# First expert layer of a two-block network on Trainium2: token rows made by one-hot products on TensorE, in place of gathers from a token store

## What is computed

```python
def _hier_moe(h, w_group, b_group, w_router, b_router, w_gate, w_up, w_down):
    ...                                       # eid: 2 experts of each token; wts: their weights
    order = jnp.argsort(eid)
    dest = pad_start[eid_s] + jnp.arange(n_asg) - start[eid_s]
    xb = h_pad[tok_buf].reshape(n_blocks, MOE_BLOCK, d)      # rows of h, expert by expert
    def expert_block(args):
        xe, e = args
        return (jax.nn.silu(xe @ w_gate[e]) * (xe @ w_up[e])) @ w_down[e]
    y = lax.map(expert_block, (xb, blk_e)).reshape(cap, d)
    out = jax.ops.segment_sum(y.astype(jnp.float32) * w_buf[:, None], tok_buf, num_segments=t + 1)
    return out[:t]
```

## Time and profile before

| | us |
|---|---|
| median of 3 runs (lowest, highest) | 2401.6 (2398.14, 2402.22) |
| span of the profiled execution, core 0 | 2400.5 |
| its whole time | not listed apart from the three runs |
| PE busy | 2173.3 (91%) |
| DVE busy | 1108.4 (46%) |
| ACT busy | 692.3 (29%) |
| POOL busy | 215.8 (9%) |
| mean granted TensorE clock | 0.952 of full |

### The profile page before, as it was taken

How to read it: one execution, slowest core, us unless ns; L and a number is a source line. 1 busy time by engine, 2 the same in 40 slices (tenths; PEclk the granted TensorE clock), 3 DMA queues, 4 the chain that set the end, 5 groups by cost and what they waited for, 6 DMA issues and landing times. The chain is left out here.

```text
span 2400.5 us, 29499 instructions
## 1 busy us (share of the span) xinstructions
PE 2173.3 (91%) x11404; PEld 1361.6 (57%) x11404; DVE 1108.4 (46%) x1760; ACT 692.3 (29%) x1102; POOL 215.8 (9%) x330
## 2 busy tenths in 40 slices
PE   7999999998899999988898888888788899999996
PEld 5778788876777888856633333333366533333332
DVE  5677655465676456577511111111587522222223
ACT  4243344344334443366111110110237111111110
POOL 2000000010000001100111111111120000000000
PEclk9989999999999999999799999998889899999998
DMA  8745576573655657501799999999830799999995
GB/s 295 260 151 190 193 235 202 184 277 135 226 206 193 211 171 248 163 2 39 301 335 401 411 409 411 406 408 411 302 84 8 299 380 428 428 428 429 428 428 230
DMA packets 175600, 656.73 MB, mean 274 GB/s; under 512 B 16295, under 2 KB 61943, under 8 KB 150288
## 3 DMA queue, kind: packets, MB, share of 16 engines
q1 hardware_dynamic: 159648, 622.65, 67.6%
q0 software_dynamic: 14032, 30.00, 4.0%
q10 hardware_dynamic: 1824, 2.73, 0.3%
HBM read 649.97 MB, written 23.79 MB: 281 GB/s over the span
## 5 line engine op out<-in xcount | busy, mean ns | idle before, releaser
L750 PE MATMUL bank<-sb_ring_rounded,sb_hT_rounded 128*128 128x512 f32 x2432 | 605.7, 397 | 18.7 <-DVE sb_ring_rounded L2045 8.4
L1382 PE MATMUL bank<-sb_ring,sb_arena 128*64 128x512 f32 x1984 | 491.1, 640 | 94.1 <-DMA sb_ring<-in_w_up 91.3
L750 PEld LDWEIGHTS bank<-sb_ring_rounded,sb_hT_rounded 128*128 128x128 f32 x2432 | 459.4, 191 | 119.5 <-issue 12.9
L1382 PEld LDWEIGHTS bank<-sb_ring,sb_arena 128*64 128x64 f32 x1984 | 152.4, 146 | 378.7 <-issue 372.9
L2045 DVE TENSOR_TENSOR sb_ring_rounded<-sb_ring,sb_ring_rounded 128x2048 fp32r<-128x2048 f32 (+1 forms) x142 | 314.9, 2258 | 112.4 <-ACT sb_ring_rounded L1516 107.4
L750 PE MATMUL bank<-sb_ring_rounded,sb_arena_rounded 128*128 128x512 f32 x1408 | 356.8, 395 | 7.6 <-DVE sb_arena_rounded L2032 7.0
L1516 ACT ACTIVATE sb_ring_rounded<-sb_ring 128x2048 fp32r<-128x2048 f32 x146 | 268.1, 1887 | 125.7 <-PE bank L750 100.1
L750 PEld LDWEIGHTS bank<-sb_ring_rounded,sb_arena_rounded 128*128 128x128 f32 x1408 | 266.1, 190 | 63.3 <-DVE sb_arena_rounded L2032 7.3
L1926 ACT ACTIVATE sb_hb<-bank 64x512 f32<-64x512 f32 x64 | 37.8, 590 | 697.4 <-PE bank L1382 697.4
L1406 PE MATMUL bank<-sb_ring,sb_arena 128*64 128x512 f32 x1008 | 233.4, 606 | 3.5 <-DVE sb_arena L2877 3.5
L2877 DVE COPY sb_arena<-bank 128x256 f32<-128x256 f32 x64 | 27.1, 424 | 319.2 <-PE bank L1393 319.1
(11 more groups left out here) (372 smaller groups left out, 2121.9 us busy)
## 6 DMA issues: line engine op xcount, KB each, us to landing
sb_ring<-in_w_down SPq DMA_DIRECT2D x63, 2048.0 KB, 22.0
sb_ring<-in_w_up SPq DMA_DIRECT2D x62, 2048.0 KB, 21.3
sb_ring<-in_w_gate SPq DMA_DIRECT2D x62, 2048.0 KB, 16.9
sb_ring<-in_w_ada SPq DMA_DIRECT2D x48, 1024.0 KB, 7.5
sb_ring<-in_ffn_w_gu SPq DMA_DIRECT2D x44, 1024.0 KB, 7.8
sb_ring<-in_xa_w_kv SPq DMA_DIRECT2D x16, 1024.0 KB, 7.3
sb_ring<-in_ffn_w_down SPq DMA_DIRECT2D x16, 1024.0 KB, 6.4
sb_ring<-in_od_w_in SPq DMA_DIRECT2D x12, 1024.0 KB, 7.7
```

The source lines that it names most:

```text
L750: ins = pe.matmul(bank[b][0:rows, :], rnd(x), rnd(w[:, k, :]), start=start and k == k0 and q == 0, stop=stop and k == k1 - 1 and q == len( ...
L1382: ins = pe.matmul(bank[2 * j + part][part * ROWS:(part + 1) * ROWS, :], mxT[:, j, k, :], w[:, k, :], start=k == 0, stop=k == KD - 1)
```

## The change

Layer 0 makes its rows as layer 1 does. The store of tokens, the gathers, their waits and the turned single steps go. The marks of layer 0 cover four token tiles: 16 places for each partition in place of 8, made in two halves, the sums of which lie in the tiles `silu` and `fix`. Each half of the 1024 columns then takes four products, not two. The tiles `bc`, `tokens`, `silu` and `fix` get a plain and a rounded name at the same address. Outputs of layer 0 are collected in `hb[0]` and `bc[1]` (the last two steps in `tokens`), since the old place is used by the resident tokens' marks. As `bc[1]` is now in use during the loop, the fills of `bc[0]` and `bc[1]` for the next layer move from the start of layer 0 into its last pair (`next_modulation`). The second index table, which was for gathers, goes in both layers. GpSimd's descriptor scratch is 4096 bytes of each partition.

```diff
+        def places_of(l):
+            return st[:, 72:80 if l else 88].rearrange("p (q s) -> p q s", s=2)
+        def marks_of(t):
+            return silu_s[:].rearrange("p k c -> p (k c)")[:, t * P:(t + 1) * P] if t < 2 else fix[:, t - 2, :]
+        def my_of(l, j, own=False):
+            if l == 1:
+                return view(6144, 2, D)[0:ROWS, j, :]
+            return tokens[0:ROWS, j, :] if own else hb[0:ROWS, 0, :] if j == 0 else bc[0:ROWS, 1, :]
...
-                    sp.wait_ge(m["rows0"], 16)
-                else:
...
-                    claim(T0)
-                    claim(T1)
-                    place_rows(0)
+                claim(T0)
+                claim(T1)
+                place_rows(l, 0)
...
-            def place_rows(i):
-                m = moe[1]
+            def place_rows(l, i):
+                m = moe[l]
                 pe.wait_ge(m["marked"], i + 1)
                 pe.sem_inc(s["passed"], 1)
                 for half in range(2):
-                    for t in range(2):
-                        ins = pe.matmul(bank[T0 + half], place_marks[:, t, 0, :, :].rearrange("p s n -> p (s n)"), hr[:, t, half * NB:(half + 1) * NB],
-                                        start=t == 0, stop=t == 1)
+                    cols = slice(half * NB, (half + 1) * NB)
+                    if l == 0:
+                        for t in range(4):
+                            ins = pe.matmul(bank[T0 + half], marks_of(t), hr[:, t, cols], start=t == 0, stop=t == 3)
+                    else:
+                        for t in range(2):
+                            ins = pe.matmul(bank[T0 + half], place_marks[:, t, 0, :, :].rearrange("p s n -> p (s n)"), hr[:, t, cols],
+                                            start=t == 0, stop=t == 1)
                     ins.then_inc(m["pe_xT"], 1)
...
-                def turn_rows(j, e, landed_rows):
-                    pe.wait_ge(m[f"rows{j}"], landed_rows * 16)
-                    pe.sem_inc(s["passed"], 1)
-                    for k in range(KD):
-                        ins = pe.transpose(bank[T0 + j][:, k * ROWS:(k + 1) * ROWS], mx[0:ROWS, j, k:D:KD], ident[0:ROWS, 0:ROWS])
-                    ins.then_inc(m["pe_xT"], 1)
-                if l == 1:
-                    turn_placed(0)
+                turn_placed(l, 0)
...
-                        if l == 0 and not (last and j == 1):
-                            turn_rows(1 - j, e + 1, i + 1 + j)
-                        if l == 1 and not last:
-                            (place_rows, turn_placed)[j](i + 1)
+                        if not last:
+                            (place_rows, turn_placed)[j](l, i + 1)
...
-                        act.dma_start(DR["tok"][t * P:(t + 1) * P, :], hr[:, t, :]).then_inc(s[f"tok_stored{t % 2}"], 16)
...
-                    zeros = cst[:, C_WIN0:C_WIN0 + P].unsqueeze(1).to_broadcast([P, 2 * KD, P])
-                    act.activation(view(0, 2 * KD, P), zeros, ACT.Copy).then_inc(s["rows_zeroed"], 1)
...
+                rows_out(0)
+                placed_turned(0)
...
-            def mark(i):
-                m = moe[1]
+            def mark(l, i):
+                m = moe[l]
+                places = places_of(l)
                 if not (isinstance(i, int) and i == 0):
                     dve.wait_ge(m["marked"], i)
                     dve.tensor_scalar(places, places, -2.0 * ROWS, None, ALU.add).then_inc(m["places"], 1)
                     dve.wait_ge(m["places"], i)
                     dve.wait_ge(m["pe_xT"], i * 4 - 2)
                 row = cst[:, C_ROW:C_ROW + ROWS].unsqueeze(1).to_broadcast([P, 8, ROWS])
-                at = places.rearrange("p q s -> p (q s)").unsqueeze(2).to_broadcast([P, 8, ROWS])
-                dve.tensor_tensor(place_marks.rearrange("p t j s n -> p (t j s) n"), row, at, ALU.is_equal).then_inc(m["equals"], 1)
-                dve.wait_ge(m["equals"], i + 1)
-                dve.tensor_tensor(place_marks[:, :, 0, :, :], place_marks[:, :, 0, :, :], place_marks[:, :, 1, :, :], ALU.add).then_inc(m["marked"], 1)
+                flat = places.rearrange("p q s -> p (q s)")
+                equal = place_marks.rearrange("p t j s n -> p (t j s) n")
+                if l == 1:
+                    dve.tensor_tensor(equal, row, flat.unsqueeze(2).to_broadcast([P, 8, ROWS]), ALU.is_equal).then_inc(m["equals"], 1)
+                    dve.wait_ge(m["equals"], i + 1)
+                    dve.tensor_tensor(place_marks[:, :, 0, :, :], place_marks[:, :, 0, :, :], place_marks[:, :, 1, :, :], ALU.add).then_inc(m["marked"], 1)
+                    return
+                for half in range(2):
+                    at = flat[:, 8 * half:8 * half + 8].unsqueeze(2).to_broadcast([P, 8, ROWS])
+                    if half:
+                        dve.wait_ge(m["equals"], i * 3 + 2)
+                    dve.tensor_tensor(equal, row, at, ALU.is_equal).then_inc(m["equals"], 1)
+                    dve.wait_ge(m["equals"], i * 3 + 2 * half + 1)
+                    to = (silu_s[:].rearrange("p k c -> p (k c)") if half == 0 else fix[:].rearrange("p t n -> p (t n)"))
+                    to = to.rearrange("p (t s n) -> p t s n", t=2, s=2)
+                    dve.tensor_tensor(to, place_marks[:, :, 0, :, :], place_marks[:, :, 1, :, :], ALU.add)\
+                       .then_inc(m["marked"] if half else m["equals"], 1)
...
-                    step(dve.tensor_scalar(places[:, :, 1], mtmp[:, 3, 64:68], float(ROWS), -float(ROWS * N_EXP), ALU.mult, ALU.add))
-                    step(dve.tensor_tensor(places[:, :, 1], places[:, :, 1], rank, ALU.add))
-                    step(dve.scalar_tensor_tensor(places[:, :, 0], whole_blocks, float(ROWS * (N_EXP - 1)), places[:, :, 1], ALU.mult, ALU.add))
-                    step(dve.tensor_scalar(places[:, :, 1], places[:, :, 0], -float(ROWS), None, ALU.add))
-                    mark(0)
+                places = places_of(l)
+                step(dve.tensor_scalar(places[:, :, 1], mtmp[:, 3, 64:64 + J], float(ROWS), -float(ROWS * N_EXP), ALU.mult, ALU.add))
+                step(dve.tensor_tensor(places[:, :, 1], places[:, :, 1], rank, ALU.add))
+                step(dve.scalar_tensor_tensor(places[:, :, 0], whole_blocks, float(ROWS * (N_EXP - 1)), places[:, :, 1], ALU.mult, ALU.add))
+                step(dve.tensor_scalar(places[:, :, 1], places[:, :, 0], -float(ROWS), None, ALU.add))
+                mark(l, 0)
...
-                dve.tensor_scalar(idx[:, 1, :], idx[:, 0, :], 1, None, ALU.logical_shift_right).then_inc(*c.up(s["idx_ready"]))
-                settle()
+                dve.sem_inc(s["idx_ready"], 1)
...
-            def gather(j, e):
-                since(pool, m["pe_xT"], e - 1)
-                apart()
-                if isinstance(e, int):
-                    pool.sem_inc(m["picked_in"], 1)
-                    at = column(1, e)
-                else:
-                    pool.tensor_copy(pick[:, 0, j:j + 1], column(1, e)).then_inc(m["picked_in"], 1)
-                    pool.wait_ge(m["picked_in"], e + 1)
-                    apart()
-                    at = pick[:, 0, j:j + 1]
-                pool.indirect_dma_start(out=mx[0:ROWS, j, :], out_offset=None, in_=DR["tok"],
-                                        in_offset=bass.IndirectOffsetOnAxis(ap=at, axis=0),
-                                        bounds_check=tiles * P - 1, oob_is_err=False).then_inc(m[f"rows{j}"], 16)
...
-                        gather(j, i * 2 + j + 2)
                     if not opening(i):
                         pool.wait_ge(m[f"stored{j}"], i * 16)
@@ -3093,12 +3056,14 @@
                         pool.sem_inc(s["y_stored"], 1)
                         for t in range(2):
                             pool.wait_ge(s[f"y_loaded{t}"], 16)
+                    if l == 0 and last and j == 1:
+                        pool.wait_ge(m["pe_xT"], i * 4 + 2)
+                        apart()
+                        next_modulation()
                     if not (opening(i) and j == 0) and not (own and j == 1):
-                        store(1 - j, i * 2 + j - 1)
-            if l == 0:
-                gather(0, 0)
-                gather(1, 1)
+                        store(1 - j, i * 2 + j - 1, last and j == 1)
...
                 fill(2, mod(l, 0, 5))
-                if l == 0:
+                if l == 1:
+                    fill(0, I["g_final_2"])
+                def next_modulation():
                     fill(0, mod(1, 0, 1))
                     fill(1, mod(1, 0, 0))
-                else:
-                    fill(0, I["g_final_2"])
-                if l == 0:
-                    pool.wait_ge(s["rows_zeroed"], 1)
-                experts(pool, c, step, l)
+                experts(pool, c, l, next_modulation)
...
-    nc = bacc.Bacc("TRN2", target_bir_lowering=False, num_devices=1)
+    nc = bacc.Bacc("TRN2", target_bir_lowering=False, num_devices=1, dynamic_dma_scratch_size=4096)
```

134 lines of the change are left out of this document (50 added, 84 removed).

## The result

The changed kernel takes 2386.64 us (median of 4 runs, 2385.80 to 2391.94) against 2399.87 for the kernel before (4 runs). The ratio is 0.9949, with a 95% interval of 0.9935 to 0.9964. It is faster, by 13.2 us between the medians and 12.2 (8.6 to 15.6) by the ratio, where 7.4 were forecast. The profiled execution took 2391.94 us, with a span of 2390.1 (2400.5 before).

What follows compares the result with a forecast made beforehand. Transfers were taken to bound layer 0's pairs (32.38 us), TensorE afterwards (30.80). Loop -11.6, start +1.9, end +2.6 and layer 1 -0.3 sum to -7.4 us: 2394.2 us from 2401.6, range 2388.5 to 2401.

Steps and rivals of the forecast that it cites:

- Other edits: Outside loop and seams: one shift less in layer 1, -0.3 us; rows of y and smaller descriptor scratch cost nothing.
- rival d: More than forecast: expert 0 starts at 1206, fills land early; -10.8 us, 2390.8 us; chance 0.12.
- The loop: Layer 0, expert 0 to expert 31: pairs of 30.80 us set by TensorE, 480.7 to 469.0 us, -11.6.
- The start: Before layer 0's expert 0: placing replaces token stores and first gather, partly at low clock; +1.9 us, range +0.9 to +2.7.
- The end: End of layer 0: VectorE waits for the moved modulation fills before the norm; +2.6 us, range +1.1 to +5.5.
- Layer 1: The index table loses a shift in layer 1, one VectorE operation before the step count: -0.3 us.
- (a): Seams of layer 0: fills land with the median or later, placing begins at low clock; -3.7 us, 2397.9; chance 0.17.
- (b): Layer 0's loop: transfers stay the bound at 31.5 us a pair; -2.4 us, 2399.2; chance 0.11.
- (c): Layer 0's loop: placing waits for marks' second half, clock falls; at 1.7 us a pair +18, 2420; chance 0.10.
- Layer 0 at 31.1: Mild form of transfers staying the bound: weights at 435 GB/s, 32 stored rows 1.1 us, layer 0's pair 31.1 us.

Runs made afterwards that it cites:

- b_scratch4k: The kernel before with only GpSimd's descriptor scratch set to 4096 bytes: 2394.3 us against 2399.06, ratio 0.9978.
- a_again: The changed kernel run once more with no edit: 2386.35 us, ratio to the kernel before 0.9953.
- the second profile: Profile of the changed kernel run again without an edit: span 2384.1 us, profiled at 2385.94 us.
- b_half_gather: The kernel before with gathers of half rows, 2 KB for each index instead of 4 KB (leaves work out): 2386.87 us in one run.
- b_no_gather: The kernel before without layer 0's gathers beyond the first two (leaves work out): 2364.72 us in one run.

## Why the prediction was wrong

**The step that failed** is in "Other edits": "GpSimd's smaller descriptor scratch costs nothing as long as only a store and two fills are outstanding". I looked for a loss only, in the loop, and put the edit at nothing. It gives 6.1 us in the profiles and 5.3 (3.1 to 7.4) by the ratio of b_scratch4k, at the end of the program, where GpSimd's drain held the exit open. The trace of before had the row: a drain of 10.48 us and 6.3 us in which SyncE waited at the exit. I read the end of expert layer 0 and never the end of the program. With this term the sum is -12.7 to -13.5, and the time moved by 12.2 to 13.2. Without it, after against before with the small scratch is 0.9949 / 0.9978, 7.0 us; with a_again, timed beside b_scratch4k, it is 6.0 by the ratios and 8.0 by the medians. The sum had 7.4. That it is so near is in part luck, since its terms missed by up to 1.5 us in both directions, as follows. The range's near end, 2388.5, was built from the terms of the expert layer alone (rival d), so it could not hold the time.

**The loop**, -11.6: -13.0 measured. The mechanism was right: bound moved to TensorE, no waits, clock 1.00, marks in time. The pair was mis-sized by 0.2 us, since placing 16 records takes 7.07 us, not twice 3.63; over 14 pairs that is 2.8. The stretch from expert 0 to expert 2 took 1.5 us more than the 26.6 of the sum (1208.21 to 1236.35), because that row was from layer 1, whose first products ran at the full clock (7.09 us) and here took 8.78. That transfers would allow 30.4 was near (30.0 to 30.3), but the reasoning under it was wrong: I shared the 2.39 us between stores and gathers at 25 ns a row, and the gathers cost nearly all of it, 35 ns a row.

**The start**, +1.9: +2.5 from the rank's reduction and +2.8 in the second profile, just past the range's +2.7; +2.2 by expert 0's own start. The first placing did run at the low clock in part: it took 8.24 us, 1.0 more than the 7.26 of the sum and not 1.8. From its end to expert 0 it took 5.2 us where 3.39 + 1.1 were summed.

**The end**, +2.6: +3.6 in the first profile, +1.4 in the second, inside the range. The wait for the fills is as described (6.79 and 5.51 us). From the issue of the first fill to VectorE's start are 7.9 us (1700.23 to 1708.10) and 7.3 in the second profile; 7.75 were taken. For one fill the Trainium skill's fit (DMA: Bandwidth & Descriptors, "Anatomy of one DMA — SWDGE (gpsimd) path") gives an estimate of 3.2 us, and this case's traces don't agree: in the first profile after, GpSimd's transfers of the tile `bc` there took 6.0 to 8.7 us to land. The second profile's +1.4 is near that fit's +1.1 for another reason: the loads of y ended 22.9 us after expert 31, against 24.4 in the first and 23.6 before.

**Layer 1**, -0.3: not seen. From the reduction of its routing to its expert 0 are 10.2 us before, and 10.3 and 10.1 after.

**Rivals.** Gain eaten at the seams (a): they took 4.3 to 6.1 us of the loop's 13.0, where 4.5 were forecast and 8.2 would have been (a). Transfers bind (b) and placing waits for marks (c) did not occur. For (c) the prediction reads that the clock falls after waits of 2 us from the earlier trace rows; the waits there are over 4 us, and after 2.47 in the earlier trace rows the products took 3.65, so that price was not in the rows named. More than forecast (d) had the right direction but neither of its reasons: the start was later and the fills did not land early. Layer 0 at 31.1 by the ceiling that the Trainium skill gives (DMA: Bandwidth & Descriptors, "Specifications") did not come: stored rows cost no time beyond their bytes.

## What to carry to other kernels

Read how the program ends: the time from the last work to the end of the span, and each engine's exit there. A setting that seems to touch only memory was worth some 5 us here, beside 13 from a loop. When two bounds lie 0.6 us apart, as TensorE's 30.6 and the transfers' 30.0 do here, relieving the one gains no more than those 0.6 before the other binds. And moving one instruction ahead of a wait gains nothing where the next wait on the same engine is as late: the fills alone gave no time that could be told apart, and the power had to move with them.

## What the hardware showed

- GpSimd's drain at the exit took 3.3 us with a descriptor scratch of 4096 bytes, 4.4 with 8192, and 9.6 to 10.5 in kernels that set no size (before and b_half_gather 10.5, b_no_gather 9.6). With the two small sizes the changed kernel ended 4.9 us after the drain's start either way.
- Rows gathered by index from device memory, 4 KB each into one partition, lengthened a pair of transfer-bound steps by 2.26 us for 0.26 MB, as if they went at 116 GB/s beside weights at 428; half rows lengthened it by 1.26. 32 more rows stored by index added 0.13 us.
- The clock of 16 products in the same place of the same kernel was low in one run and full in another (8.78 and 7.09 us for expert 0 of layer 1). A stretch with such groups of short products took 191.0 to 193.7 us by the run, so one profile can be off by 2.7 us from this.
